# Sine products of the rotary turn: swapped halves read in place by VectorE instead of being moved by transfers

## The chip, the cores and the metric

One core of a Trainium2 chip runs the whole program in one launch. The metric is the device time in microseconds; before the change it is 871.7 us (median of three runs, 871.33 to 871.93).

## The reference

The program computes two transformer blocks, one after the other, on 256 tokens of width 1024, in float32. Only the second one is touched here. It puts 16 meta tokens ahead of the 256, multiplies the normalised tokens by a wide matrix `w_in`, cuts the result into queries, keys, values and gates of two attentions (one in a window, one differential), and turns queries and keys by their position:

```
def rope(x, pos):
    ...
    x1, x2 = xf[..., :half], xf[..., half:]
    return jnp.concatenate([x1 * cos - x2 * sin, x2 * cos + x1 * sin], axis=-1)
...
qa = rope(qa, pos); ka = rope(ka, pos); qb = rope(qb, pos); kb = rope(kb, pos)
```

So each half of a head's 64 features is multiplied by a cosine, and the other half, with a sign, by a sine, and the two products are added. The attentions, gates, an output product and a gated MLP follow.

## The kernel before

Weights come as 136 blobs of 128 x 2048 float32, one after another. TensorE multiplies in a split form: ScalarE casts a blob to the high part `whi` (`hi`, L887), VectorE subtracts to get the low part `wlo` (`lo`, L1879), and each product is made of high and low parts. All engines run straight-line programs in one order written out by hand; semaphores alone keep them together.

The second block's projection has 18 blobs, `m2` = 0 to 17. Their kinds are fixed lists: five key blobs (0, 2, 4, 6, 8), eight query blobs (5, 7, 9, 10, 12, 13, 15, 17), five value blobs. `SWAPPED` is the sorted list of the first two. TensorE's order is a loop of slots `q`, two for each blob (L1784): half a blob's products, then `slot(q)`, which holds the small pieces of work of the attention. The attention works in 32 units; unit U's scores are made in slot U + 22 (L1780), that is from blob 11's first half on. TensorE waits there for `u_max`, which tells that VectorE has read the scores of the unit before. The transposes of a value blob (L1751) are in slots as well, those of blob 11 in slot 24; they wait for ScalarE's copy L1145.

The program holds the features of a key or query blob transposed: features on the 128 partitions, tokens along the free dimension (272 for keys with the meta tokens, 256 for queries, two groups of each). The weights' columns are ordered so that a head's first half lies on partitions 0 to 63 and the second half on 64 to 127. A blob's path is this:

- ScalarE copies the products out of PSUM (`keys_out`, L1111), or ScalarE copies the low part and VectorE adds the rest (`queries_low` L1119, `queries_raw` L2352). The result is `kraw[b]`, b = m2 % 2.
- SyncE issues two transfers (`swap_halves`, L806 and L807) from `kraw[b]` to `kswap[b]`: partitions 64 to 127 go to 0 to 63 and the reverse. Before that it waits for the copy and for `kt_ok`, by which GpSimd tells that it has read what `kswap[b]` held. In SyncE's order, the swap of blob m2 stands behind the load of blob m2 + 4, ahead of the stores of finished keys and queries and of the next load.
- VectorE waits for both transfers (`ks_in`) and makes three operations (`turned_keys` L2370 to L2372, `turned_queries` L2360 to L2363): `kraw` times cosine, `kswap` times sine (the sine's table has the sign, minus on the lower 64 partitions and plus on the upper), and their sum into `kswap`.
- ScalarE copies the sum to the high part (`keys_high` L1128, `queries_high` L1135, two copies for queries), GpSimd subtracts to get the low part (L1382, L1389), and SyncE stores them.

VectorE's loop over `q` (L2375) sets its order. In an even slot: the front of an attention unit if there is one (`unit_front`, L2081 to L2088, signals `u_max`), the sum of the query blob before (m2 − 1), the turn of blob m2 − 2, the back of a unit (`unit_back`, L2097 and on). In an odd slot: front, the low part of blob m2 + 2 (`lo`), back. So from slot 16 on the order is: sum 7, turn 6, lo 10, turn 7, lo 11, sum 9, turn 8, lo 12, sum 10, turn 9, front of unit 0, lo 13, back of unit 0, front of unit 1, turn 10, back of unit 1. ScalarE's order around it is: exponentials of a unit, its normalisation (L1219, after `unit_back`), the high parts of blob 9 (L1135), the copy of value blob 11 (L1145), and in even slots the cast of a blob (L887) at the end.

`link` (L478) makes an engine wait for its own instruction before the next.

Of the kernel before, what the change touches and what calls it, by code (L numbers as in the profile page):

```python
# [20 lines left out]
ALU = mybir.AluOpType  # L21
# [3 lines left out]
P = 128  # L25
D = 1024
TOK = 256
# [11 lines left out]
S_HEADS, S_KV, DH = 16, 4, 64  # L39
# [3 lines left out]
KEYS = TOK + N_META  # L43
# [71 lines left out]
SWAPPED = tuple(sorted(KEY_BLOBS + QUERIES))  # L115
# [5 lines left out]
def turned_place(m2):  # L121

    return SWAPPED.index(m2) + 1
# [9 lines left out]
    return VALUES[i]  # L133


def swaps_before(m2):

    return len([m for m in SWAPPED if m < m2 and m % 2 == m2 % 2])


def unit_place(U):
# [43 lines left out]
def build(nc, w, x, meta, consts, turns, rows, grow, out):  # L185

    with ExitStack() as ctx:
# [116 lines left out]
        kraw = [new("kraw0", [P, 2, KEYS]), new("kraw1", [P, 2, KEYS])]  # L304
        kswap = [new("kswap0", [P, 2, KEYS]), new("kswap1", [P, 2, KEYS])]
# [26 lines left out]
        turn = new("turn", [P, 2, KEYS])  # L332
# [57 lines left out]
        taken_a = sem("taken_a")  # L390
# [47 lines left out]
        kt_ok = sem("kt_ok")  # L438
# [4 lines left out]
        ks_in = [sem("ks_in0"), sem("ks_in1")]  # L443
# [34 lines left out]
        def link(eng, name, ins):  # L478

            steps[name] += 1  # L480
            ins.then_inc(chain[name], 1)
            eng.wait_ge(chain[name], steps[name])
# [17 lines left out]
        def taken_by(group):  # L500

            return 2 * TAKERS[:group + 1].count(TAKERS[group])
# [260 lines left out]
        def _(sp):  # L763
# [36 lines left out]
            def swap_halves(m2):  # L800

                sp.wait_ge(taken_d if m2 in QUERIES else taken_a, taken_by(16 + m2))
                b = m2 % 2
                if swaps_before(m2):
                    sp.wait_ge(kt_ok, max(turned_place(m) for m in SWAPPED if m < m2 and m % 2 == b))
                sp.dma_start(kswap[b][0:DH], kraw[b][DH:P]).then_inc(ks_in[b], 16)  # L806
                sp.dma_start(kswap[b][DH:P], kraw[b][0:DH]).then_inc(ks_in[b], 16)  # L807
# [44 lines left out]
            for n in range(N1, plain):  # L852
                load(n, w[n], n - 2)
                m = n - N1
                if m - 4 in SWAPPED:
                    swap_halves(m - 4)
                if m - 6 in KEY_BLOBS:
                    store_keys(KEY_BLOBS.index(m - 6))
                if m in (11, 16):
                    load_shared_keys((m - 11) // 5)  # L860
                if m == 19:
                    load_keys(0)
                if 22 <= m < 29:
                    load_keys(m - 21)
                if m == 22:
                    for t in range(NT):
                        sp.dma_start(gate_s[:, t, :], grow[5].partition_broadcast(P)).then_inc(bias_in[2], 16)
                if m - 7 in QUERIES:
                    store_queries(m - 7)
# [996 lines left out]
        def _(dve):  # L1866
# [283 lines left out]
            for n in range(MIX1):  # L2150
# [35 lines left out]
                if n in (13, 15):  # L2186
                    hh = n - 13
                    v = gr[:, hh:hh + 2]
                    for t in range(NT):
                        dve.wait_ge(e_ok, 2 * (hh // 2) + t + 1)  # L2190
                        free(dve.scalar_tensor_tensor(out=v[:, :, t, :],
                                                      in0=ps[:, (n - 13) + t, :].rearrange("p (a v) -> p a v", a=2),
                                                      scalar=stat[:, t, 3:4], in1=v[:, :, t, :], op0=ALU.mult,
                                                      op1=ALU.mult))
                if n in (17, 19, 21, 23):
# [3 lines left out]
                    for t in range(NT):  # L2199
                        v = (gate_a if g < 2 else gate_r)[:, t, half_columns(g % 2)]  # L2200
                        free(dve.scalar_tensor_tensor(out=v, in0=ps[:, 2 * (g % 2) + t, :], scalar=stat[:, t, 3:4],
                                                      in1=v, op0=ALU.mult, op1=ALU.add))
                if 18 <= n < 22:
                    r = n - 18
                    dve.wait_ge(rt_hi, 2 * r + 2)
                    for j in range(2):
                        dve.scalar_tensor_tensor(out=retT_l[:, 2 * r + j, :], in0=ps[:, 6, j * TOK:(j + 1) * TOK],
                                                 scalar=cl("ret_gn", 2 * r + j), in1=retT_h[:, 2 * r + j, :],
                                                 op0=ALU.mult, op1=ALU.subtract).then_inc(rt_lo, 1)
                if 16 <= n < 20:  # L2210
                    r = n - 16
                    b = r % 2
                    dve.wait_ge(ro_ps, r + 1)
                    for t in range(NT):
                        m = dve.bn_stats(gn_stat[:, b, t, :], ps[:, 5, t * TOK:(t + 1) * TOK])
                    link(dve, "dve", m)
                    for t in range(NT):
                        m = dve.bn_aggr(gn_mv[:, b, t, :], gn_stat[:, b, t, :])
                    m.then_inc(rv_ok, 1)
                    dve.wait_ge(rv_ok, r + 1)  # L2220
                    for t in range(NT):
                        m = dve.scalar_tensor_tensor(out=gr[:, r, t, :], in0=ps[:, 5, t * TOK:(t + 1) * TOK],
                                                     scalar=gn_mv[:, b, t, 0:1], in1=gr[:, r, t, :],
                                                     op0=ALU.subtract, op1=ALU.mult)
                    link(dve, "dve", m)
                    dve.wait_ge(rr_ok, r + 1)
                    for t in range(NT):
                        m = dve.tensor_scalar(gr[:, r, t, :], gr[:, r, t, :], gn_r[:, b, t:t + 1], None, ALU.mult)
# [8 lines left out]
                if n in (24, 25):  # L2237
                    dve.wait_ge(blob_used, n)
                    dve.wait_ge(gate_ok, n - 23)
                    for t in range(NT):  # L2240
                        v = gate_a[:, t, half_columns(n - 24)]
# [41 lines left out]
            b = MIX1  # L2283
# [8 lines left out]
            with dve.Fori(0, STEP1 - 1) as i:  # L2292
                b = MIX1 + 2
# [10 lines left out]
            b = N1 - 2  # L2304
# [26 lines left out]
            for t in range(NT):  # L2331
                for half in range(2):
                    v = h[:, t, half * BANK:(half + 1) * BANK]
                    dve.scalar_tensor_tensor(out=v, in0=v, scalar=stat[:, t, 3:4],
                                             in1=gain_row[:, half * BANK:(half + 1) * BANK], op0=ALU.mult,
                                             op1=ALU.mult).then_inc(h_ok, 1)
# [5 lines left out]
            for t in range(NT):  # L2342
                m = dve.tensor_tensor(stat[:, t, 3:4], stat[:, t, 3:4], shares_of(t, True)[:, 3:4], ALU.mult)
# [3 lines left out]
            def queries_raw(m2):  # L2347
# [3 lines left out]
                freed[0] += 2  # L2351
                dve.tensor_tensor(raw_q, ps[:, bank:bank + 2, 0:TOK], raw_q, ALU.add).then_inc(taken_d, 2)  # L2352

            def turned_queries(m2):

                b = m2 % 2
                dve.wait_ge(taken_d, taken_by(16 + m2))
                raw_q, swap_q = kraw[b][:, :, 0:TOK], kswap[b][:, :, 0:TOK]
                dve.wait_ge(ks_in[b], 32 * (swaps_before(m2) + 1))
                dve.tensor_tensor(raw_q, raw_q, turn[:, 0, 0:TOK].unsqueeze(1).to_broadcast([P, 2, TOK]), ALU.mult)  # L2360
                link(dve, "dve", dve.tensor_tensor(
                    swap_q, swap_q, turn[:, 1, 0:TOK].unsqueeze(1).to_broadcast([P, 2, TOK]), ALU.mult))
                dve.tensor_tensor(swap_q, raw_q, swap_q, ALU.add).then_inc(rot_ok, 1)  # L2363

            def turned_keys(m2):

                b = m2 % 2
                dve.wait_ge(ks_in[b], 32 * (swaps_before(m2) + 1))
                cs, sn = (turn[:, v, :].unsqueeze(1).to_broadcast([P, 2, KEYS]) for v in range(2))
                dve.tensor_tensor(kraw[b][:], kraw[b][:], cs, ALU.mult)  # L2370
                link(dve, "dve", dve.tensor_tensor(kswap[b][:], kswap[b][:], sn, ALU.mult))
                dve.tensor_tensor(kswap[b][:], kraw[b][:], kswap[b][:], ALU.add).then_inc(rot_ok, 1)  # L2372


            for q in range(2 * OUT2):  # L2375
                m2 = q // 2
# [4 lines left out]
                if q == 4:  # L2381
                    take_rows(rrow2, 2, 5)
                    for v in range(2):
                        m = dve.tensor_tensor(turn[:, v, 0:TOK], turn[:, v, 0:TOK], rrow2[:], ALU.mult)
# [4 lines left out]
                if S_UNITS <= U < UNITS:  # L2389
                    cc, t = unit_place(U)  # L2390
                    dve.wait_ge(d_hi, U + 1)
                    if U == S_UNITS:
                        dve.wait_ge(kt_ok, len(SWAPPED))
                    dve.scalar_tensor_tensor(out=dT_l[:, cc, t * P:(t + 1) * P], in0=ps[:, 5, 3 * P:4 * P],
                                             scalar=subgain[:], in1=dT_h[:, cc, t * P:(t + 1) * P],
                                             op0=ALU.mult, op1=ALU.subtract).then_inc(d_lo, 1)
# [11 lines left out]
                if q in (42, 46, 58, 62):  # L2408
# [3 lines left out]
                    for t in range(NT):  # L2412
                        v = (gate_s if g < 2 else gate_d)[:, t, half_columns(g % 2)]
# [315 lines left out]
```

## Time and profile before

| what | value |
|---|---|
| median of three runs | 871.7 us |
| the profiled execution's own time | 872.63 us |
| its span | 870.8 us |
| granted TensorE clock | 0.998 |
| busy: TensorE, its weight loads, VectorE, ScalarE, GpSimd | 860.1, 736.2, 625.8, 467.9, 70.8 us |
| swap transfers (kswap<-kraw) | 26 of 136 KB, 2.6 us to landing (median) |

PE is TensorE, PEld its weight loads, DVE VectorE, ACT ScalarE, POOL GpSimd, SP SyncE; a q behind the name is the engine's sequencer. L12 is line 12 of the kernel before. Times of a row are in us from the start of the span. The time in brackets at the end of a timeline row is how long the engine stood idle before it, and what released it. The duration of an instruction on VectorE can overlap the next one's start by some 0.1 us, as its pipeline empties.

### The profile page before, as it was taken

The page shows a single profiled execution, that of the slowest core. Times are in us where ns is not written, and L with a number is a line of the kernel's source. Part 1 is how long each engine was busy: PE and PEld are TensorE (multiplying, and loading weights), DVE is VectorE, ACT ScalarE, POOL GpSimd, SP SyncE. Part 2 cuts the span into 40 slices and gives each one's busy share as a digit, 9 for nine tenths or more (in the row PEclk, how much of TensorE's full clock was granted, in tenths as well). Part 3 has the DMA queues.
Part 4 walks back from the last instruction along what each step waited for, and adds up shares of the span by engine and source line. Part 5 has one row for each costly group of instructions (what it writes and reads, how often), then busy time and mean ns, then how long its engine had stood idle before and what let it go on. Part 6 is the DMA issues. An engine that isn't in the chain of part 4 may idle for free.

```text
span 870.8 us, 13086 instructions
## 1 busy us (share of the span) xinstructions
PE 860.1 (99%) x4812; PEld 736.2 (85%) x4812; DVE 625.8 (72%) x985; ACT 467.9 (54%) x756; POOL 70.8 (8%) x96
## 2 busy tenths in 40 slices
PE   9999999999999999999998999999999999999997
PEld 6887788888888888889997888888888888888886
DVE  6867677766876666668687887887766876666665
ACT  6546534434644444445565887676653654444443
POOL 1000010000200000002142010133300100000000
PEclk9999999999999999999999999999999999999999
DMA  9955344554565555352788535755475365455531
GB/s 330 414 206 189 121 167 148 193 184 154 186 242 193 193 193 193 145 193 64 258 273 281 164 112 173 250 188 187 156 275 173 120 239 187 175 197 188 185 142 48
DMA packets 31774, 167.21 MB, mean 192 GB/s; under 512 B 4128, under 2 KB 5920, under 8 KB 14320
## 3 DMA queue, kind: packets, MB, share of 16 engines
q1 hardware_dynamic: 29280, 160.22, 52.5%
q10 hardware_dynamic: 2448, 6.37, 2.2%
q8 instruction: 29, 0.48, 0.2%
q14 instruction: 17, 0.14, 0.1%
HBM read 157.02 MB, written 3.83 MB: 185 GB/s over the span
## 4 chain that ended last, share of the span: by engine, by line
PE 96%; DMA 2%; DVE 1%; ACT 0%; issue 0%; SPq 0%; DVEq 0%; POOL 0%; ACTq 0%
PE ps L526 18%; PE ps L528 18%; PE ps L527 18%; PE ps L692 8%; PE ps L677 8%; PE ps L696 4%; PE ps L673 4%; PE ps L705 3%; PE ps L1780 2%; PE ps L707 1%; PE ps L561 1%; PE ps L1714 1%; DMA kswap<-kraw 1%; PE ps L1738 1%; PE ps L1733 1%; PE ps L1728 1%
## 5 line engine op out<-in xcount | busy, mean ns | idle before, releaser
L1879 DVE TENSOR_TENSOR wlo<-raw,whi 128x2048 fp32r<-128x2048 f32 x134 | 306.9, 2291 | 147.7 <-ACT whi L887 147.1
L887 ACT ACTIVATE whi<-raw 128x2048 fp32r<-128x2048 f32 x134 | 256.2, 1913 | 181.3 <-PE ps L528 105.9
L526 PE MATMUL ps<-whi,xT 128*128 128x512 f32 x192 | 76.8, 400 | 0.0
L528 PE MATMUL ps<-whi,xT 128*128 128x512 f32 x192 | 75.0, 391 | 0.0
L527 PE MATMUL ps<-wlo,xT 128*128 128x512 f32 x192 | 74.8, 390 | 0.0
L1349 POOL TENSOR_TENSOR stat<-stat,cst 128x1 f32<-128x1 f32 x10 | 11.9, 1200 | 489.1 <-DVE stat L1899 260.7
L526 PE MATMUL ps<-whi,fT_h 128*128 128x512 f32 x128 | 50.2, 392 | 0.0
L528 PE MATMUL ps<-whi,fT_l 128*128 128x512 f32 x128 | 49.8, 389 | 0.0
L527 PE MATMUL ps<-wlo,fT_h 128*128 128x512 f32 x128 | 49.8, 389 | 0.0
L526 PE MATMUL ps<-x_all,whi 128*128 128x272 f32 x160 | 46.4, 290 | 0.0
L527 PE MATMUL ps<-x_all,whi 128*128 128x272 f32 x160 | 46.1, 288 | 0.0
L528 PE MATMUL ps<-x_all,wlo 128*128 128x272 f32 x160 | 46.1, 288 | 0.0
L1184 ACT ACTIVATE sc<-sc,usoft 128x272 f32<-128x272 f32 x64 | 32.7, 512 | 20.7 <-DVE usoft L2090 16.2
L528 PEld LDWEIGHTS ps<-whi,xT 128*128 128x128 f32 x192 | 36.0, 188 | 7.8
L526 PEld LDWEIGHTS ps<-whi,xT 128*128 128x128 f32 x192 | 36.1, 188 | 7.4
L527 PEld LDWEIGHTS ps<-wlo,xT 128*128 128x128 f32 x192 | 36.1, 188 | 7.0
L677 PE MATMUL ps<-x_all,whi 128*128 128x512 f32 x176 | 42.0, 391 | 0.0
L526 PE MATMUL ps<-whi,x_all 128*128 128x512 f32 x96 | 38.0, 396 | 0.0
L692 PE MATMUL ps<-x_all,whi 128*128 128x512 f32 x160 | 38.0, 390 | 0.0
L528 PE MATMUL ps<-whi,x_all 128*128 128x512 f32 x96 | 37.7, 393 | 0.0
L677 PEld LDWEIGHTS ps<-x_all,whi 128*128 128x128 f32 x176 | 32.3, 188 | 6.3
L527 PE MATMUL ps<-wlo,x_all 128*128 128x512 f32 x96 | 37.6, 391 | 0.0
(349 smaller groups left out, 1876.4 us busy)
## 6 DMA issues: line engine op xcount, KB each, us to landing
raw<-weights SPq DMA_DIRECT2D x134, 1024.0 KB, 4.8
kB<-key_parts SPq DMA_DIRECT2D x20, 272.0 KB, 3.3
kswap<-kraw SPq DMA_DIRECT2D x26, 136.0 KB, 2.6
key_parts<-knat SPq DMA_DIRECT2D x4, 544.0 KB, 5.1
cst<-consts SPq DMA_DIRECT2D x1, 1371.0 KB, 13.3
raw<-weights SPq DMA_DIRECT2D x4, 256.0 KB, 5.6
raw<-weights SPq DMA_DIRECT2D x2, 512.0 KB, 7.0
gate_a<-gain_rows ACTq DMA_DIRECT2D x2, 512.0 KB, 8.0
```

The lines of the kernel that those rows point to most:

```text
L526: pe.matmul(o, lh, rh, start=first, stop=False)
L527: pe.matmul(o, lh, rl, start=False, stop=False)
L528: return pe.matmul(o, ll, rh, start=False, stop=last)
L673: pe.matmul(ps[:, bank0 + j, 0:TOK], vl[:, k, j * P:(j + 1) * P], x[:, 0, k, :], start=k == 0, stop=False, skip_group_check=True)
L677: m = pe.matmul(ps[:, bank0 + j, :], vh[:, k, j * P:(j + 1) * P], x[:, :, k, :], start=False, stop=k == KC - 1, skip_group_check=True)
L692: pe.matmul(ps[:, bank0 + j, :], vh[:, k, j * P:(j + 1) * P], x[:, :, k, :], start=k == 0, stop=False)
L696: m = pe.matmul(ps[:, bank0 + j, 0:TOK], vl[:, k, j * P:(j + 1) * P], x[:, 0, k, :], start=False, stop=k == KC - 1)
L705: pe.matmul(ps[:, bank + j, :], vh[:, k, j * P:(j + 1) * P], x2[:, :, k, :], start=k == 0, stop=False)
L887: act.activation(whi[s][:], raw[s][:], ACT.Copy).then_inc(split_hi, 1)
L1184: ins = act.activation(scores(U, u), scores(U, u), ACT.Exp, bias=st[:, 2, u:u + 1], accum_out=st[:, 4, u:u + 1])
L1780: m = pe.matmul(ps[:, 4 + u, 0:KEYS], qT[u][:, cc, t * P:(t + 1) * P], kT[:, 2 * u + v, 0:KEYS].bitcast(F32R), start=v == 0, stop=v == 1)
L1879: dve.tensor_tensor(wlo[s][:], raw[s][:], whi[s][:], ALU.subtract).then_inc(split_lo, 1)
```

## The change

For the nine key and query blobs below 11 (`HELD`) no transfer is made. VectorE makes the sine product itself: for each half of the partitions one scalar_tensor_tensor reads `kraw` and the sine table on the other half, multiplies them and by −1 (the sine table's sign is that of the partitions it is read from), and writes to this half of `kswap`. Its two instructions work on 64 partitions each and cover all columns; they stand ahead of the cosine product now, since that overwrites `kraw`, and the cosine product waits for them. The wait for `kt_ok` moves from SyncE to VectorE for these blobs. The query blobs 12, 13, 15 and 17 keep their transfers, and keep the order sine product, cosine product, sum (new for them too: the sine product now comes first).

```
+HELD = tuple(m2 for m2 in SWAPPED if m2 < 11)
...
 def swaps_before(m2):
-    return len([m for m in SWAPPED if m < m2 and m % 2 == m2 % 2])
+    return len([m for m in SWAPPED if m < m2 and m % 2 == m2 % 2 and m not in HELD])
...
-                if swaps_before(m2):
+                if any(m < m2 and m % 2 == b for m in SWAPPED):
                     sp.wait_ge(kt_ok, max(turned_place(m) for m in SWAPPED if m < m2 and m % 2 == b))
...
-                if m - 4 in SWAPPED:
+                if m - 4 in SWAPPED and m - 4 not in HELD:
                     swap_halves(m - 4)
...
+            def crossed(m2, width):
+                b = m2 % 2
+                if any(m < m2 and m % 2 == b for m in SWAPPED):
+                    dve.wait_ge(kt_ok, max(turned_place(m) for m in SWAPPED if m < m2 and m % 2 == b))
+                for a in (0, DH):
+                    of = slice(DH - a, P - a)
+                    m = dve.scalar_tensor_tensor(out=kswap[b][a:a + DH, :, 0:width], in0=kraw[b][of, :, 0:width], scalar=-1.0,
+                                                 in1=turn[of, 1, 0:width].unsqueeze(1).to_broadcast([DH, 2, width]),
+                                                 op0=ALU.mult, op1=ALU.mult)
+                link(dve, "dve", m)
...
             def turned_queries(m2):
                 b = m2 % 2
                 dve.wait_ge(taken_d, taken_by(16 + m2))
                 raw_q, swap_q = kraw[b][:, :, 0:TOK], kswap[b][:, :, 0:TOK]
-                dve.wait_ge(ks_in[b], 32 * (swaps_before(m2) + 1))
-                dve.tensor_tensor(raw_q, raw_q, turn[:, 0, 0:TOK].unsqueeze(1).to_broadcast([P, 2, TOK]), ALU.mult)
+                if m2 in HELD:
+                    crossed(m2, TOK)
+                else:
+                    dve.wait_ge(ks_in[b], 32 * (swaps_before(m2) + 1))
+                    dve.tensor_tensor(swap_q, swap_q, turn[:, 1, 0:TOK].unsqueeze(1).to_broadcast([P, 2, TOK]), ALU.mult)
                 link(dve, "dve", dve.tensor_tensor(
-                    swap_q, swap_q, turn[:, 1, 0:TOK].unsqueeze(1).to_broadcast([P, 2, TOK]), ALU.mult))
+                    raw_q, raw_q, turn[:, 0, 0:TOK].unsqueeze(1).to_broadcast([P, 2, TOK]), ALU.mult))
                 dve.tensor_tensor(swap_q, raw_q, swap_q, ALU.add).then_inc(rot_ok, 1)
...
             def turned_keys(m2):
                 b = m2 % 2
-                dve.wait_ge(ks_in[b], 32 * (swaps_before(m2) + 1))
-                cs, sn = (turn[:, v, :].unsqueeze(1).to_broadcast([P, 2, KEYS]) for v in range(2))
-                dve.tensor_tensor(kraw[b][:], kraw[b][:], cs, ALU.mult)
-                link(dve, "dve", dve.tensor_tensor(kswap[b][:], kswap[b][:], sn, ALU.mult))
+                dve.wait_ge(taken_a, taken_by(16 + m2))
+                crossed(m2, KEYS)
+                link(dve, "dve", dve.tensor_tensor(
+                    kraw[b][:], kraw[b][:], turn[:, 0, :].unsqueeze(1).to_broadcast([P, 2, KEYS]), ALU.mult))
                 dve.tensor_tensor(kswap[b][:], kraw[b][:], kswap[b][:], ALU.add).then_inc(rot_ok, 1)
```

## Rows read from the trace of the kernel before

**Rows 1.** The page, part 1: busy time, share of the span, instructions.
```profile
PE 860.1 (99%) x4812; PEld 736.2 (85%) x4812; DVE 625.8 (72%) x985; ACT 467.9 (54%) x756; POOL 70.8 (8%) x96
```

**Rows 2.** Waits of TensorE: who waited for whom, us in total, times, longest.
```profile
PE ps L1751 <- ACT kraw L1145: 1.4, 1, 1.4
PE ps L1780 <- DVE usoft L2088: 1.3, 1, 1.3
```

**Rows 3.** Timeline of TensorE, 470 to 486 us: start, duration, instruction, idle before.
```profile
470.29 0.77 PE L1780 MATMUL ps<-kB,qs 128*128 128x272 f32 x4 [1.28 <-DVE usoft L2088]
...
475.28 0.44 PE L1751 MATMUL ps<-cst,kraw 128*128 128x128 f32 x2 [1.42 <-ACT kraw L1145]
...
484.63 0.60 PE L1714 MATMUL ps<-cst,sc 128*128 128x128 f32 x4
```

**Rows 4.** The chain that ended last, 452 to 480 us: start, duration, piece.
```profile
458.89 8.12 DMA kswap<-kraw
...
470.24 2.20 DVE wlo L1879
```

**Rows 5.** Timeline of VectorE, 434 to 478 us.
```profile
435.04 0.72 DVE L2370 TENSOR_TENSOR kraw<-kraw,turn 128x544 f32<-128x544 f32 x1
...
437.06 2.29 DVE L1879 TENSOR_TENSOR wlo<-raw,whi 128x2048 fp32r<-128x2048 f32 x1
439.83 1.29 DVE L2360 TENSOR_TENSOR kraw<-kraw,turn 128x512 f32<-128x512 f32 x1 [0.48 <-DMA kswap<-kraw]
...
443.76 2.29 DVE L1879 TENSOR_TENSOR wlo<-raw,whi 128x2048 fp32r<-128x2048 f32 x1 [1.24 <-ACT whi L887]
...
454.41 2.28 DVE L1879 TENSOR_TENSOR wlo<-raw,whi 128x2048 fp32r<-128x2048 f32 x1
457.64 0.69 DVE L2352 TENSOR_TENSOR kraw<-ps,kraw 128x512 f32<-128x512 f32 x1 [0.94 <-ACT kraw L1119]
...
467.10 0.69 DVE L2360 TENSOR_TENSOR kraw<-kraw,turn 128x512 f32<-128x512 f32 x1 [2.81 <-DMA kswap<-kraw]
467.71 0.68 DVE L2361 TENSOR_TENSOR kswap<-kswap,turn 128x512 f32<-128x512 f32 x1
468.43 0.69 DVE L2363 TENSOR_TENSOR kswap<-kraw,kswap 128x512 f32<-128x512 f32 x1
469.04 0.43 DVE L2081 CUSTOM_DVE_ANT_0 sc<-ps,cst 128x272 f32<-128x272 f32 x1
...
470.07 0.16 DVE L2088 TENSOR_TENSOR usoft<-usoft,negsink 128x2 f32<-128x2 f32 x1
...
475.05 1.65 DVE L2363 TENSOR_TENSOR kswap<-kraw,kswap 128x512 f32<-128x512 f32 x1
476.63 0.15 DVE L2097 TENSOR_TENSOR usoft<-usoft 128x2 f32<-128x2 f32 x1
```

**Rows 6.** Timeline of VectorE, 403 to 407 us, four instructions merged.
```profile
403.77 2.74 DVE L2334 SCALAR_TENSOR_TENSOR h<-h,stat,gain_row 128x512 f32<-128x512 f32 x4 [0.54 <-POOL stat L1349]
```

**Rows 7.** Timeline of GpSimd, 434 to 480 us.
```profile
437.92 2.65 POOL L1382 TENSOR_TENSOR knat<-kswap,knat 128x544 fp32r<-128x544 f32 x1 [9.73 <-ACT knat L1128]
...
455.76 2.10 POOL L1389 TENSOR_TENSOR ql<-kswap,qs 128x512 fp32r<-128x512 f32 x1 [3.14 <-ACT qs L1135]
...
474.79 1.37 POOL L1389 TENSOR_TENSOR ql<-kswap,qd 128x512 fp32r<-128x512 f32 x1 [9.96 <-ACT qd L1135]
```

**Rows 8.** Timeline of all engines, 582 to 584 us.
```profile
582.93 0.50 DVE L2104 SCALAR_TENSOR_TENSOR sc<-sc,usoft 128x272 f32<-128x272 f32 x1
583.07 0.41 POOL L1339 TENSOR_SCALAR ostat<-ostat 128x1 f32<-128x1 f32 x1 [2.82 <-ACT o_tok L1214]
```

**Rows 9.** Instructions of line L1339: durations in ns, least, median, most.
```profile
L1339 POOL TENSOR_SCALAR ostat<-ostat x16: 190/191/1222, 561.4 to 625.9; 128x1 f32<-128x1 f32 x16
```

**Rows 10.** Timeline of ScalarE, 450 to 484 us.
```profile
465.83 1.92 ACT L887 ACTIVATE whi<-raw 128x2048 fp32r<-128x2048 f32 x1 [2.71 <-DMA raw<-weights]
...
482.38 0.94 ACT L1219 ACTIVATE sc<-sc,usoft 128x272 f32<-128x272 f32 x2 [0.24 <-DVE usoft L2098]
```

## The prediction

> **What bounds the kernel now.** I read the page's busy line first: TensorE is busy 860.1 of 870.8 us [rows 1], so only time in which it stands still can be won back cheaply. The view of waits, cut to TensorE, comes second: six waits in all, and the two that this change can reach are the 1.3 us before L1780 and the 1.4 us before L1751 [rows 2]; the others belong to the start and to the residual sum. TensorE's timeline gives their places: 1.28 us end at 470.29, 1.42 us at 475.28 [rows 3]. Their sum, 2.70 us, is the ceiling of any gain. Third, the chain of waits tells what stood ahead of them [rows 4]: a swap transfer of 8.12 us, from 458.89 to 467.01, then VectorE's work, then blob 13's low half at 470.24. Last, VectorE's own timeline [rows 5]: the turn of blob 9 starts at 467.10, after 2.81 us idle for that transfer; the front of the first attention unit follows at 469.04 and ends at 470.07 + 0.16 = 470.23, and TensorE's L1780 starts 0.06 later. I call that end T. From T to the start of L1751 it is 475.28 − 470.23 = 5.05 us of fixed order (split, unit back, normalisation, query copies, the copy that L1751 waits for). So both stalls hang on T = 470.23, and the question is when T comes if no transfer is awaited.
>
> **The change part by part.** It removes the transfers of nine blobs (0, 2, 4 to 10), two of each, and the wait for them. It replaces one tensor_tensor product over 128 partitions by two scalar_tensor_tensor (STT) products over 64, and puts the cosine product behind them with one more wait.
>
> *Price of an STT.* The trace has no STT over 64 partitions, nor any VectorE operation whose input and output stand in different partitions. The nearest row is L2334, same operation, both tensors in SBUF, 512 elements: four in 2.74 us, one alone 0.75, so 0.66 from one start to the next [rows 6]. Below, half the partitions might take half the time (0.38); above, the crossing might cost a second pass (1.50). I take 0.75, the nearest row, since its length in elements is the same; for 544 elements 0.78, as a tensor_tensor grows from 0.69 to 0.72 between these sizes [rows 5].
>
> *Price of a turn.* A key turn takes 435.04 to 437.06, 2.02 us; a query turn 467.10 to 469.04, 1.94 [rows 5]. Inside it a product that the next one needn't wait for costs 0.61 (467.10 to 467.71), one that it must wait for its length and 0.04 (467.71 + 0.68 to 468.43). The edit takes away the first kind (0.64 for keys, 0.61 for queries) and adds one STT at its spacing (0.70 or 0.66) and one with the wait behind it (0.78 or 0.75, plus 0.04). That makes 2.02 + 0.88 = 2.90 and 1.94 + 0.84 = 2.78.
>
> *GpSimd in between.* After each turn ScalarE copies it and GpSimd subtracts. The row of 437.92 lasts 2.65 and ends at 440.57 [rows 7], 1.22 after the end of VectorE's L1879 (437.06 + 2.29 = 439.35) during which it was issued; the one of 455.76 ends 1.17 after L1879's end (456.69). Conversely VectorE's product issued at 439.83, while GpSimd was at work, lasted 1.29 and ended 0.55 after GpSimd; that of 475.05 lasted 1.65 and ended 0.54 after GpSimd's 476.16. So they exclude each other, and a blocked product ends its own duration less 0.14 after GpSimd. The sums L2352, which read PSUM, run at full length beside GpSimd (0.69 at 457.64, while the work of 455.76 runs to 457.86). Today the transfer's wait mostly covers GpSimd's turn; afterwards it stands in the open, because GpSimd always asks during the L1879 that follows a turn, and comes before the next STT: asking at 474.79, while a product ran, it came before the one of 475.05.
>
> Is an STT excluded too? At 582.93 one with both inputs in SBUF runs to 583.43, and GpSimd's L1339, usually 0.191, is stretched to 0.41 and ends 0.05 after it [rows 8, 9]. I take it that it is. The Trainium skill (SBUF — State Buffer, Who interferes with whom) says the same of any VectorE operation with two SBUF inputs against a GpSimd operation that reads SBUF; by that the sum below stands, and the first rival falls.
>
> *The sum.* From one L1879 to the next: L1879 2.28, GpSimd's rest, then the turn with its first STT blocked (0.13 less than a free one). A query turn behind GpSimd's key subtraction: 2.28 + 1.22 + 2.65 = 6.15. A key turn behind its query subtraction: 2.28 + 1.17 + 2.77 = 6.22, with L2352 beneath GpSimd. Blob 4's turn starts at 435.04 as now. Then: 435.04 + 2.90 (turn 4) = 437.94; + 6.15 (to the split after turn 5) + 0.10 (the small lambda operation) = 444.19, against 443.76 now; + 6.22 = 450.41; + 6.15 = 456.56; + 6.22 = 462.78; + 6.15 = 468.93, the start of the front; + 1.19 (its length, 469.04 to 470.23) = **470.12**. That is 0.11 before today's T. What the transfers' waits give back, 2.81 us of it ahead of blob 9's turn alone, goes to twelve STTs and five blocked starts. TensorE's two stalls stay within 0.1 us of what they are.
>
> The Trainium skill (VectorE: DVE Perf Modes, Two Vector instructions with no wait between them) has a rule against the change: an instruction that reads from or writes to another quadrant of partitions than the one ahead starts only when the earlier ones have finished. No row here shows it; by it, with the overlap of 0.08 gone in six turns, the sum would be 0.5 higher.
>
> *What is added elsewhere.* The new wait for GpSimd (kt_ok) moves from SyncE to VectorE. Behind it on VectorE stand the split and the front, and TensorE waits for those. It is free: the turn of blob 9 needs GpSimd's work on blob 7, which the sum ends at 456.56 + 2.28 + 1.17 = 460.0, against 465 when it is asked; the others are asked for later still behind theirs. SyncE loses 18 issues and its waits, so weights are issued earlier; nothing is won, since ScalarE's cast of blob 13 ends at 465.83 + 1.92 = 467.75 today [rows 10], before T. The splits come up to 2.1 us later (456.56 against 454.41 for blob 11's), ahead of TensorE by over 3 us still. The turn of blob 10 lies behind T. It ends at 476.63 today with a blocked product [rows 5]; it is blocked once afterwards too, so the pair of STTs adds its 0.84. ScalarE's normalisation, which ends at 482.38 + 0.94 = 483.32 [rows 10], would end at 484.2, before TensorE's next work of that unit at 484.63 [rows 3]: hidden, by 0.5 us; without that cover it costs at most 0.84.
>
> Against the profiled execution's 872.63 (span 870.8) the sum gives 872.5; the runs' median lies 0.9 lower, so I forecast 871.7 − 0.1 = **871.6 us**.
>
> **The rivals.**
> 1. *STTs are not excluded by GpSimd.* For it: the only STT row is against a tiny GpSimd operation. Against: that row was stretched to the STT's end. VectorE would then be bound by TensorE's deliveries, the last at 457.64 (L2352 of blob 9): + 0.61 + 2.90 + 2.28 + 0.61 + 2.78 + 1.19 gives T = 468.0, 2.2 earlier. The first stall goes (1.28). TensorE, which needs 475.28 − 1.42 − 470.29 = 3.57 from L1780 to L1751, would reach L1751 at 470.29 − 1.28 + 3.57 = 472.58, and could start it at 468.0 + 5.05 = 473.05, so 0.47 of the second is left. Gain 2.2: 869.5.
> 2. *Half the partitions are cheaper.* At 0.38 each, twelve STTs take off 4.4 us, both stalls vanish, and the cap applies: 869.0. For it nothing in the rows.
> 3. *Crossing partitions costs extra: slower.* The place is the same VectorE chain, the price twelve times the surplus. From 0.15 us each the kernel loses more than 1.74; at 0.20 T is 2.4 later and TensorE waits for it at L1780: 874.0. For it: no row shows a crossing, and nothing in the chain can give way once L1879 and GpSimd alternate without a gap. Against: a 0.75 us operation has no obvious place for it.
>
> **How the numbers follow.** Forecast 0.66; rival 1 0.17; rival 2 0.05; rival 3 0.12. What a measurement of this kernel can tell is about 0.2%, 1.74 us. Rivals 1 and 2 gain more, minus a little of rival 1 that falls short, plus a little of the forecast with a cheaper STT: faster 0.21. Rival 3: slower 0.12. Rest 0.67. The forecast's own range is 870.9 to 872.4 (0.06 us per STT either way). Reaching over rival 1 and halfway into rival 3, the range is 869.4 to 873.0; the ends with 0.38 and 1.50 stay outside.
>
> **What would show it.** Right: no swap transfer before 480 us; STTs at 0.75 to 0.80; GpSimd's subtractions ending 1.2 after L1879's end and each turn's first STT lasting about 1.3 to 1.9; the front's end near 470.1; TensorE's two waits still there. Wrong: STTs at their plain length while GpSimd works (rival 1), or a front that ends before 468.5 or after 472.

## The result, and the profile after

The changed kernel takes 873.08 us (median of 22 runs, 872.29 to 875.91) against 871.85 for the kernel before (22 runs beside it, 870.81 to 872.73): ratio 1.0015, 95% interval 1.0009 to 1.0020. A second comparison gave 1.0013 (1.0004 to 1.0022). So it is 1.2 us slower: inside the 0.2% that I had called no change, but 1.5 above the forecast and just above the top of the range. The profiled execution took 872.68 (span 870.9).

First the page: busy time and instructions by engine, against [rows 1], and then each engine's share of the chain that ended last:

```profile
PE 859.5 (99%) x4812; PEld 736.2 (85%) x4812; DVE 634.7 (73%) x994; ACT 467.7 (54%) x756; POOL 71.8 (8%) x96
...
PE 90%; DVE 6%; ACT 2%; issue 1%; DMA 0%; DVEq 0%; POOL 0%; SPq 0%; ACTq 0%
```

The second of these lines for the kernel before:

```profile
PE 96%; DMA 2%; DVE 1%; ACT 0%; issue 0%; SPq 0%; DVEq 0%; POOL 0%; ACTq 0%
```

VectorE has nine more instructions (two STTs for one product in nine turns) and 8.9 us more busy time, in which time blocked by GpSimd counts. The chain that ended last no longer leads through a swap transfer; VectorE's share of it has grown from 1% to 6%. TensorE's waits (line, who ended the wait: us in total, times, longest), against [rows 2]:

```profile
PE ps L1754 <- ACT kraw L1148: 2.1, 2, 1.4
...
PE ps L1783 <- DVE usoft L2091: 1.1, 1, 1.1
```

L1783 is the L1780 of before, L1754 its L1751. The stall before the scores has gone from 1.28 to 1.12; the wait before the transposes of value blobs comes **twice** now, where [rows 2] had it once. VectorE's timeline shows that the part up to the end of the front came out as worked out; it answers to [rows 5]:

```profile
433.82 0.69 DVE L2355 TENSOR_TENSOR kraw<-ps,kraw 128x512 f32<-128x512 f32 x1 [1.50 <-ACT kraw L1122]
434.54 1.45 DVE L2364 SCALAR_TENSOR_TENSOR kswap<-kraw,turn 64x544 f32<-64x544 f32 x2
436.03 0.72 DVE L2388 TENSOR_TENSOR kraw<-kraw,turn 128x544 f32<-128x544 f32 x1
...
437.43 2.28 DVE L1882 TENSOR_TENSOR wlo<-raw,whi 128x2048 fp32r<-128x2048 f32 x1
439.75 2.44 DVE L2364 SCALAR_TENSOR_TENSOR kswap<-kraw,turn 64x512 f32<-64x512 f32 x2
...
443.62 2.29 DVE L1882 TENSOR_TENSOR wlo<-raw,whi 128x2048 fp32r<-128x2048 f32 x1
...
464.35 0.68 DVE L2355 TENSOR_TENSOR kraw<-ps,kraw 128x512 f32<-128x512 f32 x1
465.06 1.84 DVE L2364 SCALAR_TENSOR_TENSOR kswap<-kraw,turn 64x512 f32<-64x512 f32 x2
...
469.31 0.16 DVE L2091 TENSOR_TENSOR usoft<-usoft,negsink 128x2 f32<-128x2 f32 x1
...
473.07 1.39 DVE L2364 SCALAR_TENSOR_TENSOR kswap<-kraw,turn 64x512 f32<-64x512 f32 x2
474.49 1.65 DVE L2379 TENSOR_TENSOR kraw<-kraw,turn 128x512 f32<-128x512 f32 x1
476.18 0.69 DVE L2381 TENSOR_TENSOR kswap<-kraw,kswap 128x512 f32<-128x512 f32 x1
```

An x2 row is both STTs of a turn. A pair of STTs that nothing blocks lasts 1.45 (544 elements) or 1.39 (512); one whose first half is blocked by GpSimd 1.84 to 2.45. The front ends at 469.31 + 0.16 = 469.47. GpSimd's subtractions end behind the L1882 during which they were asked for, as in [rows 7]: 438.29 + 2.65 is 1.23 after the end of L1882, 437.43 + 2.28.

```profile
438.29 2.65 POOL L1385 TENSOR_TENSOR knat<-kswap,knat 128x544 fp32r<-128x544 f32 x1 [9.67 <-ACT knat L1131]
474.03 1.57 POOL L1392 TENSOR_TENSOR ql<-kswap,qd 128x512 fp32r<-128x512 f32 x1 [8.38 <-ACT qd L1138]
```

The second row lies in the turn of blob 10 and stretches its cosine product (474.49) to 1.65; before, it was the sum of that turn that was stretched as much [rows 5]. ScalarE's timeline behind that turn, against [rows 10]:

```profile
477.18 0.94 ACT L1222 ACTIVATE sc<-sc,usoft 128x272 f32<-128x272 f32 x2 [0.94 <-DVE usoft L2101]
...
482.55 0.94 ACT L1222 ACTIVATE sc<-sc,usoft 128x272 f32<-128x272 f32 x2 [0.23 <-DVE usoft L2101]
...
503.88 0.60 ACT L1148 ACTIVATE kraw<-ps 128x544 f32<-128x544 f32 x1
```

The same stretch of the kernel before:

```profile
477.01 0.94 ACT L1219 ACTIVATE sc<-sc,usoft 128x272 f32<-128x272 f32 x2
...
503.92 0.60 ACT L1145 ACTIVATE kraw<-ps 128x544 f32<-128x544 f32 x1
```

The rows at 477 are the normalisation of unit 1, which follows the turn of blob 10; that at 482.55 is of unit 2. Before, the normalisation of unit 1 starts without a pause; after, ScalarE waits 0.94 for VectorE. And 27 us later ScalarE copies value blob 14 at nearly the same time as before (503.88 and 503.92), though everything at 470 was 0.77 earlier. TensorE's rows say what that means; after:

```profile
504.54 0.44 PE L1754 MATMUL ps<-cst,kraw 128*128 128x128 f32 x2 [0.67 <-ACT kraw L1148]
```

and before:

```profile
504.19 0.40 PE L707 MATMUL ps<-x_all,wlo 128*128 128x256 f32 x2
504.58 0.44 PE L1751 MATMUL ps<-cst,kraw 128*128 128x128 f32 x2
```

Before, TensorE reached these transposes just when the copy was done (503.92 + 0.60 = 504.52); after, it stands for 0.67. The chain that ended last, in order of time, has no TensorE in it between 433.07 and 504.54; VectorE and ScalarE hand over to each other:

```profile
432.10 0.97 PE ps L710 x8
433.09 0.61 ACT kraw L1122
...
476.98 0.17 DVE usoft L2101
...
478.11 1.81 ACT whi L890
...
479.95 2.29 DVE wlo L1882
...
497.56 1.81 ACT whi L890
...
499.40 2.29 DVE wlo L1882
...
502.93 1.04 ACT qs L1138 x2
503.98 0.52 ACT kraw L1148
...
504.54 0.44 PE ps L1754 x2
```

### The profile page after: what moved, and what is told of

It reads as the page before. It is cut to its first block, busy times and chain, and to the rows that moved or that the text cites. A ratio compares the mean times of both kernels' runs of the same rounds, so it can differ in the third digit from the quotient of the medians.

```text
span 870.9 us, 13073 instructions
## 1 busy us (share of the span) xinstructions
PE 859.5 (99%) x4812; PEld 736.2 (85%) x4812; DVE 634.7 (73%) x994; ACT 467.7 (54%) x756; POOL 71.8 (8%) x96
## 4 chain that ended last, share of the span: by engine, by line
PE 90%; DVE 6%; ACT 2%; issue 1%; DMA 0%; DVEq 0%; POOL 0%; SPq 0%; ACTq 0%
PE ps L529 18%; PE ps L531 17%; PE ps L530 17%; PE ps L695 8%; PE ps L680 8%; PE ps L699 4%; PE ps L676 4%; DVE wlo L1882 2%; PE ps L1783 2%; DVE kswap L2364 2%; PE ps L564 1%; PE ps L708 1%; PE ps L1717 1%; PE ps L1741 1%; ACT whi L890 1%
## 5 line engine op out<-in xcount | busy, mean ns | idle before, releaser
L1882 DVE TENSOR_TENSOR wlo<-raw,whi 128x2048 fp32r<-128x2048 f32 x134 | 306.8, 2291 | 145.6 <-ACT whi L890 145.1
```

The source lines that it names most:

```text
L1882: dve.tensor_tensor(wlo[s][:], raw[s][:], whi[s][:], ALU.subtract).then_inc(split_lo, 1)
```

## Experiments

All ratios are to the kernel before, run beside it on the same chip, with 95% intervals.

**One blob at a time.** The list HELD was made free to choose: a blob outside it keeps its transfers and a plain product.

```
no10:    HELD = tuple(m2 for m2 in SWAPPED if m2 < 10)
only10:  HELD = (10,)
only9:   HELD = (9,)
none:    HELD = ()
h89:     HELD = (8, 9)      (below)
```

> The changed kernel, but blob 10 keeps its two swap transfers and its plain product. Theory (the surplus of blob 10's turn, 0.9 us, is carried along VectorE and ScalarE and stops TensorE for 0.67 us before the transposes of value blob 14, at 504.5): that stall is gone or under 0.1, the front of attention unit 0 still ends near 469.5, TensorE's stalls before it stay at 1.1 to 1.4, and the time comes back to that of the kernel before or 0.2 under it (ratio 0.9995 to 1.0003). Rival (the 1.2 us between the medians come from the other eight blobs, or from the start): ratio stays at 1.0010 to 1.0015.

> The kernel before, with the change made for blob 10 alone (sine product first in the other turns, by plain products on transferred halves). Theory: the front of unit 0 ends as before (470.2 in the profiled execution), and the stall before the transposes of value blob 14 appears with 0.6 to 0.8 us: ratio 1.0006 to 1.0010. Rival (the other blobs cause the loss): no stall there, ratio 0.9998 to 1.0003.

> The kernel before, with the change made for blob 9 alone, whose transfers VectorE awaits for 2.81 us. Theory (what the transfers' wait gives back is eaten by the STTs and by GpSimd's subtractions in the earlier turns, not by the change of blob 9): the turn of blob 9 starts behind the sum at 464.2, is blocked by GpSimd until 464.8, ends at 467.5; the front of unit 0 ends at 468.7, 1.5 earlier; TensorE's stall before the scores (1.28) goes to 0 and the one before the transposes of value blob 11 is about 1.1; ratio 0.9981 to 0.9986. Rival (VectorE and ScalarE behind unit 0 hold TensorE back anyway, as at 504.5 in the changed kernel): part of the 1.5 comes back as a stall between 484 and 506, ratio 0.9990 to 1.0000.

> The changed kernel with an empty list of blobs: all halves swapped by transfers, only the order of the two products turned round (sine first, the cosine product waiting for it). Both theories: as the kernel before, ratio 0.9998 to 1.0002, stalls of 1.3 and 1.4, none at 504.5. If it were slower, the order or the new wait would carry part of the loss.

Measured: no10 872.43, 1.0006 (0.9998 to 1.0015); only10 872.06, 1.0005 (0.9996 to 1.0013); only9 870.75, 0.9990 (0.9981 to 0.9999); none 871.61, 0.9997 (0.9988 to 1.0006). The stall at 504.5 follows blob 10: it is there with only10,

```profile
504.85 0.44 PE L1754 MATMUL ps<-cst,kraw 128*128 128x128 f32 x2 [0.67 <-ACT kraw L1148]
```

and gone with no10:

```profile
503.70 0.44 PE L1754 MATMUL ps<-cst,kraw 128*128 128x128 f32 x2
```

So the place of that loss is settled by where the stall appears and where it does not. The times don't part the theories: both ratios lie between what theory and rival had. no10 did not come down to the kernel before as expected. The order of the products (none) costs nothing that shows. In the trace of only9 the first STT, blocked by GpSimd, stands at 463.84 where a transfer was awaited until 467.10 before, TensorE's wait before the scores is gone, and no other wait takes its place between 484 and 506:

```profile
468.30 0.77 PE L1783 MATMUL ps<-kB,qs 128*128 128x272 f32 x4
```

```profile
463.84 1.84 DVE L2364 SCALAR_TENSOR_TENSOR kswap<-kraw,turn 64x512 f32<-64x512 f32 x2
```

Its front ends at 468.24 (expected 468.7); the stall before value blob 11 is 1.42, not 1.1, since TensorE also arrived earlier. Its ratio of 0.9990 is above the 0.9981 to 0.9986 of the theory, at the rival's edge; the interval holds both.

**Is it the length of blob 10's turn?** pad10 keeps all transfers and adds a plain product there; narrow9 is the changed kernel with GpSimd's subtraction for blob 9, which falls into that turn, cut to 16 columns.

```
pad10:    + HELD = ()
          + if m2 == 10: link(dve, "dve", dve.tensor_tensor(raw_q, raw_q, raw_q, ALU.max))
narrow9:  + w = 16 if m2 == 9 else TOK
          - pool.tensor_tensor(ql[i % 2][:], kswap[..., 0:TOK], ...)
          + pool.tensor_tensor(ql[i % 2][:, :, 0:w], kswap[..., 0:w], ...)
```

> The kernel with all halves swapped by transfers and the sine product first, and one more plain product on VectorE in the turn of blob 10 (each element's larger of itself and itself, which changes nothing): 0.61 to 0.72 us more there. Theory (it is the length of that turn that is carried to 504.5, 0.27 of it being absorbed on the way): a stall of 0.35 to 0.45 before the transposes of value blob 14. Rival (the stall has to do with the STTs or the missing transfers of blob 10): none there.

> The changed kernel, with GpSimd's subtraction for blob 9 alone cut to 16 columns (the rest of that low half is left out). It is the one that falls into the turn of blob 10 and stretches a product there to 1.65. Theory (that length is what reaches TensorE): the product lasts 0.69, the turn is 0.9 shorter, ScalarE waits under 0.1 before the normalisation near 477, and the stall before value blob 14 is gone, with the two earlier stalls at 1.12 and 1.43. Rival (the stall there comes from elsewhere in the changed kernel): 0.6 to 0.7 again.

pad10, ScalarE's normalisation and then TensorE's transposes:

```profile
478.16 0.94 ACT L1222 ACTIVATE sc<-sc,usoft 128x272 f32<-128x272 f32 x2 [0.86 <-DVE usoft L2101]
```

```profile
505.51 0.44 PE L1754 MATMUL ps<-cst,kraw 128*128 128x128 f32 x2 [0.57 <-ACT kraw L1148]
```

ScalarE waits 0.86 and TensorE 0.57, without one STT in the turns (0.35 to 0.45 was expected; the turn grew from the 2.90 of none to 3.75: 0.72 by the product and its wait, and 0.13 more because GpSimd now blocked the cosine product, for which the sum must wait, and not the sum itself). Of 0.94 there arrive 0.67, of 0.86 there arrive 0.57: 0.27 to 0.29 is absorbed on the way. narrow9, its turn of blob 10, ScalarE's normalisation and TensorE's transposes:

```profile
472.74 1.39 DVE L2365 SCALAR_TENSOR_TENSOR kswap<-kraw,turn 64x512 f32<-64x512 f32 x2
474.17 0.69 DVE L2380 TENSOR_TENSOR kraw<-kraw,turn 128x512 f32<-128x512 f32 x1
```

```profile
475.89 0.94 ACT L1222 ACTIVATE sc<-sc,usoft 128x272 f32<-128x272 f32 x2
```

```profile
503.54 0.44 PE L1755 MATMUL ps<-cst,kraw 128*128 128x128 f32 x2
```

With the product at 0.69, ScalarE doesn't wait at the normalisation (475.89) and the stall is gone, while the two others are 1.12 and 1.42. So it is the length of this turn, whatever makes it up, that reaches TensorE 30 us later.

**What ate the removed waits?** narrow cuts GpSimd's subtractions for blobs 0 to 9 to 16 columns; aligned lets each STT read its own half, so the swap is left out.

```
narrow:   - pool.tensor_tensor(knat[i % 2][:, :, 1], kswap[m2 % 2][:], ...)
          + pool.tensor_tensor(knat[i % 2][:, :, 1, 0:16], kswap[m2 % 2][:, :, 0:16], ...)   (queries alike; the rest set to 0)
aligned:  - of = slice(DH - a, P - a)
          + of = slice(a, a + DH)
```

> The changed kernel, with GpSimd's subtractions for blobs 0 to 9 cut to 16 columns (the rest of these low halves is set to zero by GpSimd, so this part of the computation is left out). Theory (what the removed waits gave back went to GpSimd's turns, which exclude VectorE's): the first product of each turn lasts 0.7 instead of 1.1 to 1.75, the front of unit 0 ends 2.0 us earlier than in the changed kernel (467.4), TensorE's stall before the scores goes to 0, the one before value blob 11 to 0.5, and the one at 504.5 stays near 0.7; ratio to the kernel before 0.9988 to 0.9994. Rival (VectorE's own length sets the place, GpSimd's turns lie in slack): front within 0.3 of the changed kernel, ratio 1.0010 to 1.0015.

> The changed kernel, but each half of the sine product reads its own partitions instead of those 64 away (the swap is left out). Theory (crossing has no price): the products last the same 0.72 and 0.69, the front of unit 0 ends within 0.1 of the changed kernel, stalls 1.1, 1.4 and 0.7 at the same places. Rival (crossing has a price): they last shorter, 0.05 or more each, and the front ends 0.6 or more earlier.

narrow took 870.26, ratio 0.9986 (0.9977 to 0.9995), by the two ratios 2.5 less than the changed kernel, with the same STTs (by the traces 0.67 of it is the stall at 504.5, which is gone too). GpSimd out of the way, VectorE does in its turn of blob 5:

```profile
439.84 1.39 DVE L2370 SCALAR_TENSOR_TENSOR kswap<-kraw,turn 64x512 f32<-64x512 f32 x2
```

1.39 for the pair in place of 2.44, the front ends at 467.61 instead of 469.47, and the stall before the scores is gone. I had expected 0.5 before value blob 11 (0.88 came), and wrongly that the stall at 504.5 would stay: blob 9's subtraction was cut too, which by narrow9 is enough.

In aligned the turn of blob 4, which GpSimd does not block, begins like this:

```profile
435.34 0.69 DVE L2355 TENSOR_TENSOR kraw<-ps,kraw 128x512 f32<-128x512 f32 x1 [1.51 <-ACT kraw L1122]
435.94 1.44 DVE L2364 SCALAR_TENSOR_TENSOR kswap<-kraw,turn 64x544 f32<-64x544 f32 x2
```

The pair lasts 1.44 against 1.45 with the crossing, so crossing does not make an STT longer. But here the pair starts 0.60 after the sum ahead of it, with the crossing 0.72 (433.82 to 434.54), and the stall before the scores is 1.00 in place of 1.12. So crossing has a price after all, 0.12 where a turn starts free behind a sum; where GpSimd blocks the start it is hidden: from the sum ahead to the cosine product of blob 9 both kernels take 2.59 (after: 464.35 to 466.94). The stalls of aligned at the two other places are 1.42 and 0.59; its 873.96 (one run) is due to a late arrival of TensorE, as the table below shows.

**The base of the forecast.** The two kernels were run again as they are, and no10 too.

> The kernel before, profiled a second time. Theory (the execution from which the prediction was worked out was a late one in the term that decides: its swap transfer of blob 9 landed late, so that the sum of 470.12 was set against a late 470.23): the scores of unit 0 wait less than 1.28 us here, about 0.5 to 0.9, as in the two runs above that keep that transfer. Rival (1.28 is usual, and the rest of the loss lies in the start): 1.2 to 1.4 again.

> The kernel before, profiled a third time, for the same question: 0.5 to 0.9 by the theory, 1.2 to 1.4 by the rival. The gap of TensorE near 7 to 8 us, at the start, varies by some tenths in either case.

> The kernel before, profiled a fourth time, for the spread of the stall before the scores: 1.28, 0.82 and 1.24 so far; with the two others that keep blob 9's transfers (0.86, 0.50) its mean is 0.94. Both theories: between 0.5 and 1.3; no stall at 504.5.

> The changed kernel, profiled a second time. Theory: its three stalls repeat, as nothing in them hangs on a transfer: 1.1 before the scores, 1.4 before value blob 11, 0.6 to 0.7 before value blob 14. Rival (chance of one execution): the third is missing or differs by over 0.2.

> The kernel before, timed as if it were a changed one, against the runs of the kernel before on the same chip: what the comparison makes of no change. Both theories: ratio 0.9996 to 1.0004; its profiled execution has a stall of 0.5 to 1.3 before the scores and none at 504.5.

> The changed kernel, timed a second time. Theory (the two stalls are all): ratio 1.0008 to 1.0011, that is 0.7 to 0.95 us; stalls 1.12, 1.43 and 0.67 as in both of its profiles. Rival (a further 0.4 us is lost in a place that a comparison of single profiles doesn't show): 1.0013 to 1.0017.

> The changed kernel with blob 10 left on its transfers, timed a second time on the chip of after_again. Theory: ratio to the kernel before 1.0000 to 1.0003, and 0.67 us under after_again; rival: 1.0006 or more.

before_again 871.31, ratio 1.0000 (0.9991 to 1.0009); after_again 872.72, 1.0013 (1.0004 to 1.0022); no10_again 872.29, 1.0011 (1.0002 to 1.0020). The last two went with their rivals, and no10_again is 0.43 under after_again, not 0.67; the intervals are too wide to exclude the theory. The profiled executions side by side: when TensorE arrives at the scores of unit 0 (start less idle), how long it then stands there, before value blob 11 and before value blob 14, the profiled time, and what is left of it after arrival and stalls:

```
                 arrives  scores  blob11  blob14   time    rest
before           469.01   1.28    1.42    0       872.63  400.92
before2          468.83   0.82    1.42    0       872.05  400.98
before3          468.67   1.24    1.43    0       872.32  400.98
before4          468.37   0.80    1.44    0       871.58  400.97
before_again     468.74   1.16    1.42    0       872.29  400.97
none             469.38   0.50    1.43    0       872.18  400.87
only10           468.99   0.86    1.45    0.67    872.96  400.99
pad10            469.90   0.68    1.42    0.57    873.58  401.01
after            468.40   1.12    1.43    0.67    872.68  401.06
after2           469.21   1.12    1.45    0.67    873.44  400.99
after_again      468.11   1.13    1.42    0.65    872.35  401.04
no10             468.23   1.12    1.42    0       871.85  401.08
no10_again       467.94   1.13    1.42    0       871.53  401.04
aligned          469.92   1.00    1.42    0.59    873.96  401.03
narrow9          468.07   1.12    1.42    0       871.63  401.02
only9            468.30   0       1.42    0       870.63  400.91
h89              468.26   0       1.34    0       870.52  400.92
narrow           468.34   0       0.88    0       870.11  400.89
```

The rest is 401.0 within 0.13 in all 18, so to that width arrival and three stalls are the whole of each difference between profiles. Two things follow. The arrival scatters by 2 us (467.94 to 469.92), and nearly all of that arises in the first 11 us, which the change doesn't touch: TensorE's second group of `wlo` products starts at 9.85 in no10_again and at 11.91 in pad10. By then it has waited 0.41 to 1.06 for constants and up to 1.05 for its first weights, and in pad10 and aligned two of its first 128x128 products took 0.63 in place of 0.38; why, no run tells. And the stall before the scores scatters in the eight executions that wait for blob 9's transfers, from 0.50 to 1.28, mean 0.92; the execution from which I worked has the largest of the eight. In the six executions of after, no10 and narrow9 it is 1.12 or 1.13 each time. before2, before4, before_again and after2 met the expectation, before3 (1.24) went with the rival.

**A better version.** h89 holds blobs 8 and 9.

> The kernel before, with the change for blobs 8 and 9 only. Theory (GpSimd's turn sets the pace wherever a transfer is no longer waited for): the turn of blob 8 needn't wait for its transfer, ends some 0.3 earlier than with blob 9 alone, GpSimd's subtraction of it too, and the front of unit 0 ends 0.3 earlier; no stall before the scores, about 1.1 before the transposes of value blob 11, none at 504.5; ratio to the kernel before 0.9978 to 0.9988. Rival (the further blobs that the change holds are what cost time, through the two STTs of each): front later than with blob 9 alone, ratio 0.9990 to 1.0000.

870.66, ratio 0.9988 (0.9979 to 0.9997), front end at 467.99. By the ratios it beats both kernels; that it beats only9 isn't shown by the times (their intervals overlap), though its front ends 0.25 earlier (0.3 was expected), its stall before value blob 11 is 0.08 less (1.34, where 1.1 was expected) and TensorE waits nowhere else there:

```profile
473.04 0.44 PE L1754 MATMUL ps<-cst,kraw 128*128 128x128 f32 x2 [1.34 <-ACT kraw L1148]
```

## Why the prediction was wrong

**What held.** *The prices.* An STT pair without GpSimd takes 1.49 to the next product's start (434.54 to 436.03) where 0.70 + 0.82 = 1.52 was put, and 1.42 (473.07 to 474.49) for 1.45. Each STT is shorter than I took it (0.69 and 0.72), but the second starts 0.01 after the first has ended, with none of the overlap of 0.08 that [rows 5] show between plain products. The rule which the prediction cited from the Trainium skill says so for an instruction that starts in another quadrant of partitions than the one ahead (VectorE: DVE Perf Modes, Two Vector instructions with no wait between them). The traces agree with it, in aligned too: there the second STT also starts in other partitions than the first and keeps that spacing, while the first, which starts in those of the sum ahead, starts 0.09 before that sum has ended (435.34 + 0.69 against 435.94); the crossed one starts 0.03 after it (433.82 + 0.69 against 434.54). The sum did not grow by the 0.5 that I had put to that rule, because each STT is shorter by 0.06. *GpSimd excludes STTs*, as the prediction took from one row: blocked pairs last up to 2.45, and narrow makes them 1.39. The Trainium skill (SBUF — State Buffer, Who interferes with whom) has it so, and the traces agree. Rival 1 falls; a front nearly as early as the one it had (by 2.2 us) comes when GpSimd is taken away instead: 1.86 earlier in narrow. *The sum.* From the turn of blob 4 to the front's end I had 470.12 − 435.04 = 35.08; it took 469.47 − 434.54 = 34.93. The steps from one L1882 to the next were 6.19, 6.20, 6.14 and 6.19 for 6.15 and 6.22. Rival 2 falls with the lengths; of rival 3's surplus, aligned leaves 0.12 once, not twelve times.

**The step that failed** is the one on what lies behind T: "hidden, by 0.5 us; without that cover it costs at most 0.84". The row that I took for the cover, at 482.38 [rows 10], is the normalisation of unit 2; the one behind the turn of blob 10 is that of unit 1, at 477.01. Unit 2's ended at 482.55 + 0.94 = 483.49, or 484.26 on the clock of before (the arrival and the shorter stall put this execution 0.77 earlier there), as forecast (484.2), and TensorE's next work did not wait, for unit 1 or for unit 2. But that cover hides the lag from this one consumer and does not end it. VectorE and ScalarE had no pause between 477 and 504 long enough to make up the lag: it went from the normalisation into the cast (478.02), the split (479.95), the next normalisations, to the copy of value blob 14. There TensorE had come just in time before, so 0.67 of 0.94 was paid, within the 0.84 that I had put to the case without cover. only10, no10, pad10 and narrow9 show it from four sides.

**The second step** is the comparison with one profiled execution: "the runs' median lies 0.9 lower, so I forecast 871.7 − 0.1". That subtracts the 0.9 from both kernels alike. But a part of it was the wait that the change removes: 1.28 in the execution that I read, 0.92 on the mean of eight. What replaces it is 1.12 each time. Against the mean the change loses 0.2 where I had it gain 0.11. This term rests on traces alone.

Together 0.67 + 0.20 = 0.87 of the 1.2 measured; the interval (0.8 to 1.7) holds it at its lower end. The rest, some 0.3, isn't settled. no10, which has no stall at 504.5, is 0.5 to 1.0 above the kernel before by its two ratios, where the stalls explain 0.2. Either the transfers' wait is shorter in the runs of which no trace is kept than in the eight seen, or the kernels that hold eight or nine blobs lose a few tenths in those runs that their traces don't have. The record has a sign of each. For before, before_again, none and only10, which wait for blob 9's transfers, the execution with the trace is 0.57 to 0.98 slower than the median of the same kernel's own runs; for after, after_again, no10 and no10_again it is 0.37 to 0.76 faster, for only9, h89 and narrow 0.12 to 0.15 faster. So the traces put before and after 0.05 apart (872.63 and 872.68) where the medians are 1.2 apart. The arrival of a single execution, which scatters by 2 us, is part of that; how much of the open 0.3 belongs to which, no run tells.

**What the change could have won** is in only9 and h89: of the waits for transfers, the one ahead of blob 9's turn was the one that reached TensorE. Holding blobs 0 to 7 as well (no10 against h89) fills VectorE with STTs and blocked starts, so that blob 9's turn, free of its transfer, ends nearly as late as before and the stall before the scores is 1.12 where h89 has none; holding blob 10 adds the stall at 504.5.

## What to carry to other kernels

When work is added behind the point that one argues from, it is not enough that the next consumer has slack: follow the lag along the engines that carry it until a pause swallows it, and look at every later place where the bound engine arrives without a pause. Before a forecast is set against one execution, ask whether the wait that the change touches varies between executions; a median that differs from the profile isn't the same offset for a kernel without that wait. Replace a transfer by work only where the wait for the transfer reaches the engine that bounds the kernel.

## What the runs showed that was not expected

The three stalls of the changed kernel, which awaits no transfer there, repeat to 0.03 us over executions whose arrival differs by 1.1. An STT on 64 partitions lasts what a plain product of the same length lasts on 128 (0.69 for 512 elements, 0.72 for 544), so half the partitions save nothing. A swap of halves leaves that length as it is, and costs only 0.12 at the start of the turn of blob 4. And GpSimd's exclusion depends on what it does. In narrow, a memset on GpSimd ran its 0.50 in the middle of VectorE's product at 443.25, while the small subtraction behind it lasted 0.88 and ended at 445.65, 0.11 after that product:

```profile
443.25 2.29 DVE L1888 TENSOR_TENSOR wlo<-raw,whi 128x2048 fp32r<-128x2048 f32 x1 [0.50 <-ACT whi L891]
```

```profile
444.31 0.50 POOL L1396 MEMSET ql<- 128x480 f32 x1 [4.39 <-ACT qs L1139]
444.77 0.88 POOL L1398 TENSOR_TENSOR ql<-kswap,qs 128x32 fp32r<-128x32 f32 x1
```

So the price of a subtraction there is not its 16 columns, but the wait for VectorE.
